# FFN stages: where ScalarE and VectorE split the coming weight blocks, inside the up loop and through its last turns

## The reference, cut to what matters

```python
def conv_ffn(h, w_up, conv_w, conv_b, w_down):
    u = h @ w_up                                  # 1024 -> 5632 columns
    u = lax.conv_general_dilated(u, conv_w[:, None, :], window_strides=(1,),
                                 padding=[(CONV_WIDTH - 1, 0)], ...) + conv_b   # width 3, per channel
    a, b = u[..., :D_FF], u[..., D_FF:]           # D_FF = 2816
    return (jax.nn.silu(a) * b) @ w_down          # 2816 -> 1024

x = x + conv_ffn(rms_norm_2(x, ffn_norm[l]), w_up[l], conv_w[l], conv_b[l], w_down[l])
```

## Time and profile before

| what | value |
|---|---|
| time, median of 3 runs | 1364.01 us (1361.56 to 1366.23) |
| the profiled execution's own time | 1362.08 us |
| its span, first to last instruction | 1360.2 us |
| mean granted TensorE clock | 0.912 |
| PE / PEld busy | 85% / 79% of the span |
| DVE / ACT / POOL busy | 70% / 51% / 9% |
| first FFN, about | 797 to 992 us from the span's start |
| second FFN, about | 1152 to 1347 us |

### The profile page before, as it was taken

One profiled execution on the slowest core, in us unless ns is written; L12 is line 12 of the kernel. 1 busy time (PEld: TensorE's weight loads), 2 busy tenths in 40 slices (PEclk: granted clock), 3 DMA queues, 4 the chain that ended last, 5 costly groups with the idle time before them and its releaser, 6 DMA issues.

```text
span 1360.2 us, 24905 instructions
## 1 busy us (share of the span) xinstructions
PE 1153.7 (85%) x10397; PEld 1071.4 (79%) x10397; DVE 945.8 (70%) x1723; ACT 697.5 (51%) x1256; POOL 118.2 (9%) x126
## 2 busy tenths in 40 slices
PE   6799866888899669579957799998978859999986
PEld 6688765888788659577945699998977849999886
DVE  5787955667879646676768668877558476778852
ACT  5642256546422465545437656565434464565551
POOL 2000000110000001141000011110011001011100
PEclk9999976989899869889958999998988979999988
DMA  8332111344321005425510145554634303454550
GB/s 337 118 111 77 64 63 32 120 159 148 124 94 66 32 5 191 147 73 195 175 62 1 63 156 183 162 183 161 219 112 159 124 1 127 153 182 162 173 182 31
DMA packets 24448, 167.55 MB, mean 123 GB/s; under 512 B 2704, under 2 KB 2832, under 8 KB 8208
## 3 DMA queue, kind: packets, MB, share of 16 engines
q1 hardware_dynamic: 24336, 165.96, 35.1%
HBM read 164.90 MB, written 1.05 MB: 122 GB/s over the span
## 4 chain that ended last, share of the span: by engine, by line
PE 42%; DVE 35%; ACT 16%; issue 5%; DMA 1%; POOL 1%; POOLq 0%; DVEq 0%; SPq 0%; ACTq 0%
DVE WL L381 8%; PE ps L427 8%; PE ps L422 8%; PE ps L424 8%; DVE ARENA L2033 5%; DVE FR L381 4%; ACT WH L368 4%; PE ps L445 3%; PE ps L453 2%; PE ps L447 2%; ACT ARENA L745 2%; ACT FR L368 2%; PE ps L643 2%; DVE ARENA L2025 2%; ACT L484 2%
## 5 line engine op out<-in xcount | busy, mean ns | idle before, releaser
L381 DVE TENSOR_TENSOR WL<-raw,WH 128x1024 fp32r<-128x1024 f32 (+4 forms) x225 | 262.9, 1191 | 138.0 <-ACT WH L368 137.5
L422 PE MATMUL ps<-FR,WH 128*128 128x256 f32 x1248 | 310.9, 288 | 26.4 <-ACT WH L368 20.4
L424 PE MATMUL ps<-FR,WH 128*128 128x256 f32 x1248 | 307.4, 286 | 1.9 <-POOL FR L501 1.0
L368 ACT ACTIVATE WH<-raw 128x1024 fp32r<-128x1024 f32 (+4 forms) x225 | 217.5, 989 | 111.2 <-PE ps L427 64.4
L422 PEld LDWEIGHTS ps<-FR,WH 128*128 128x128 f32 x1248 | 244.1, 196 | 32.0 <-ACT WH L368 17.8
L424 PEld LDWEIGHTS ps<-FR,WH 128*128 128x128 f32 x1248 | 243.8, 195 | 4.4 <-POOL FR L501 2.1
L422 PE MATMUL ps<-FR,FR 128*128 128x256 f32 x680 | 170.3, 287 | 6.9 <-ACT FR L368 6.3
L427 PE MATMUL ps<-FR,WL 128*128 128x256 f32 x1248 | 170.6, 279 | 0.3 <-DVE WL L381 0.3
L424 PE MATMUL ps<-FR,FR 128*128 128x256 f32 x680 | 169.2, 286 | 0.2 <-DVE FR L493 0.2
L381 DVE TENSOR_TENSOR FR<-raw,FR 128x1024 fp32r<-128x1024 f32 (+2 forms) x100 | 117.2, 1193 | 73.5 <-ACT FR L368 73.5
L427 PEld LDWEIGHTS ps<-FR,WL 128*128 128x128 f32 x1248 | 156.6, 190 | 0.6 <-DVE WL L381 0.6
(11 more groups left out here) (309 smaller groups left out, 1789.7 us busy)
## 6 DMA issues: line engine op xcount, KB each, us to landing
raw<-wst_in SPq DMA_DIRECT2D x124, 1024.0 KB, 5.0
raw<-wst_in SPq DMA_DIRECT2D x14, 768.0 KB, 4.3
raw<-wst_in SPq DMA_DIRECT2D x11, 896.0 KB, 4.8
raw<-wst_in SPq DMA_DIRECT2D x4, 968.0 KB, 4.7
raw<-wst_in SPq DMA_DIRECT2D x2, 912.0 KB, 4.6
cst<-cst_in SPq DMA_DIRECT2D x1, 1681.0 KB, 15.3
X<-xT_in SPq DMA_DIRECT2D x2, 512.0 KB, 6.4
ARENA<-memT_in SPq DMA_DIRECT2D x1, 1024.0 KB, 4.8
```

Of the source, the lines that this page charges most:

```text
L368: a.activation(hi[:, 0:cols], src, ACT.Copy).then_inc(*put("split_hi", ("hi", i)))
L381: v.tensor_tensor(lo[:, 0:cols], src, hi[:, 0:cols].bitcast(F32), SUB).then_inc(*put("split_lo", ("lo", i)))
L422: pe.matmul(out, hv[:, k, :], src.hi[:, c, :], start=k0 == 0 and k == ks[0], stop=False)
L424: pe.matmul(out, hv[:, k, :], src.lo[:, c, :], start=False, stop=False)
```

## The change

Inside the up loop ScalarE's two roundings of a turn are taken apart. Apart from the first call ahead of turn 0, which stays as it was, one item (2i+7) is rounded right behind the centre taps of turn i, ahead of `part_hi` and silu (`ahead` is 4 there), and the other (2i+8) at the end of the turn. VectorE's two remainders stand at the end of turn i instead of the beginning of turn i+1, which is the same place in its queue. The calls are no longer limited to i < 22: through new marks of the plan after each of the first four products of down, turns 21 to 24 go on to split items 49 and 50, 51 and 52, 53 and 54, 55 and 56, in the same two places of ScalarE's turn.

```diff
@@ def ffn_pe(l)
             for c in range(4):
                 feat("w_down_2", l, r(128 * c, 128 * c + 128), m.F, ("F", l), first[c][:, 0:256], "down1", l, c, kc=FC, span=span)
+                if span[0] == 0:
+                    B.at_items["up", l, FC + c] = len(B.plan)
@@ def ffn_v(v, q, l)
         for i in range(FC + 3):
             if i < FC:
-                split_lo(v, q, "up", l, i)
                 if i == 0:
+                    split_lo(v, q, "up", l, i)
                     barrier(q, "V", ("P", l))
...
                 part_lo(v, q, "part_lo_v", m.F, ("F", l), n, m.fb[n % 3])
+            split_lo(v, q, "up", l, min(i + 1, FC + 3))
@@ def ffn_a(a, q, l)
         for i in range(FC + 3):
             if i < FC:
-                split_hi(a, q, "up", l, i)
                 if i == 0:
+                    split_hi(a, q, "up", l, i)
                     barrier(q, "A", ("P", l))
...
                                  bias=vcol("conv_b_2", l, c), scale=vcol("conv_w_2", l, 88 + c)).then_inc(*put("ffn_a", ("centre", l, i)))
+            split_hi(a, q, "up", l, min(i + 1, FC + 3), ahead=NW + NMORE - 2)
             if 0 <= i - 2 < FC:
...
                 a.activation(u, u, ACT.Silu).then_inc(*put("ffn_a", ("silu", l, n)))
+            split_hi(a, q, "up", l, min(i + 1, FC + 3))
```

## The result

The changed kernel takes 1350.11 us (median of 4 runs, 1348.27 to 1353.01) against 1363.7 before (4 runs): a ratio of 0.990, 95% interval 0.988 to 0.993. The forecast was 1349.2 in 1341 to 1356. Its profiled execution has a span of 1347.2 us, 13.0 less than before.

A forecast was written before the change was run, and what follows sets the result against it. The prediction took TensorE's wait for item 49 behind each up loop, and the low clock after it, as the bound. Gaining 7.4 us in each FFN, 14.8 together, brings 1364.0 to 1349.2 us, range 1341 to 1356.

The forecast's parts named there:

- The place of the loss: Behind the up loop, TensorE waits 5.31 us for item 49, then runs at clock 0.55; 5.55 us wait in second FFN.
- The wait for `part_hi`: In each loop turn VectorE's `part_lo` waits 0.70 to 0.80 us, starting at 3.10 behind u instead of 2.30.
- The product's cost: In each loop turn GpSimd's product, no longer in VectorE's idle time, costs VectorE 0.50 us, making the period 6.21.
- rival 1: In the loop, the product costs VectorE nothing: period 5.71, 10.6 us gained in each FFN, 1342.8 us; chance 0.22.
- Who comes first: In the loop, GpSimd's product starts at 3.46 behind u, 0.03 us behind the start of VectorE's first remainder.
- rivals 2 and 3: In the loop: product costs more, 1353.4 or 1358.4 us, chance 0.18; product holds up both remainders, 1373.6 us, chance 0.04.
- Where item 49 stands: Rounded in turn 21 at u(21) + 2.8, item 49 ends 7.4 us earlier: 4.9 earlier start, 2.5 clock.
- The tail: Behind item 49 in down, nothing stops TensorE: items 50 onward are ready with margins of 1 to 3 us.
- rival 4: Behind the loop, TensorE stops at items 50 to 53, turn 22 being longer; half the gain goes, 1356.6 us; chance 0.06.
- The sum: Over the whole kernel, 7.4 us gained in each FFN, 14.8 together, everything else unchanged: median 1349.2 us.

The follow-up runs named there:

- e2: The changed kernel with the middle rounding alone, without the further splitting of items in turns 21 to 24: 1366.6 us, ratio 1.002.
- e1: The changed kernel without the middle rounding: both roundings stay together at the end of ScalarE's turn, splitting goes on through turns 21 to 24: 1344.9 us, 0.986.
- e3: The changed kernel with the middle rounding moved behind `part_hi`, in front of silu: 1340.5 us, ratio 0.983.
- e4: The changed kernel with GpSimd's product waiting for the turn's second remainder, so that it runs beside u: 1339.7 us, ratio 0.982.
- e6: The changed kernel with each GpSimd product computed twice into the same place: 1349.3 us, ratio 0.989.
- e7: The changed kernel with the splitting going on in turn 21 only, not in turns 22 to 24: 1360.0 us, ratio 0.997.
- e5: The changed kernel with both the middle rounding behind `part_hi` and the product beside u: 1340.4 us, ratio 0.983.

## Why the prediction was right

**The place of the loss.** Right: the stall in front of item 49 and the low clock behind it were what the change could win. e2 keeps both and gains nothing, e1 removes them and gains more than the whole change.

**The wait for `part_hi`.** Forecast 0.70 to 0.80 us, measured 0.72, `part_lo` at 3.10 behind u as forecast. e3 takes it away.

**The product's cost.** The term 0.50 measured 1.76 - 1.22 = 0.54, and made the period 6.26 instead of 6.21. That it had to be paid at all was read from two places of the trace before that lie outside the ordinary turns of the loop. e4 shows that the cost goes when the product is moved away from the remainders, and e6 that a second product beside u is free. Without it rival 1 would have been the forecast, 1342.8, 7 us too low; its period of 5.71 is what e4 shows, 5.72, where the product is out of the way.

**Who comes first.** The forecast put GpSimd 0.03 us behind the first remainder; it was 0.01. The tie went the same way in each of the 40 turns from 2 to 21 of the two FFNs, by 0.00 to 0.01 us, and rivals 2 and 3 did not come about. Had GpSimd been first, the cost would, as an estimate from the earlier trace rows, have been about the same; no run of the loop shows that order.

**Where item 49 stands.** It is rounded by u(21) + 2.8, as forecast. Mis-sized: the gain up to item 49 is 6.04 us, not 7.4. It starts 3.89 us earlier, where 4.9 was forecast: 19 x 0.05 = 0.95 of that is the period. And it takes 3.11 us (938.56 to 941.67) instead of 2.8. The wait for its remainder is at most 0.1 of these 0.3: its last eight matmuls take 1.17 us, those of item 2 took 1.10. The forecast put 2.8, the step from the end of one item to the end of the next, for the time from first start to last end; item 47, which also begins behind a short wait, takes 3.13. TensorE had caught up with the roundings at item 37, not 41.

**The tail.** Right that TensorE waits nowhere behind item 49 in down: the stretch to item 67 takes 45.0 us, against 44.5 before. e7 puts a price on a stop there, the outcome of rival 4 though from another cause: 5.1 us a stage without the splits of turns 22 to 24.

**The sum.** 14.8 us were forecast. The two stages give 12.2 up to item 49 (6.04 and 6.14), the spans 13.0, the medians 13.6. That the total is nearer to the forecast than its terms is luck. Most of what the stages do not give lies in one place between the two FFNs, from the last matmuls of line 643 to item 2 of the second FFN: 1159.26 - 1123.63 = 35.63 us before, 1152.93 - 1119.05 = 33.88 in the changed kernel, with another granted clock in its first 8 us. First PE and the stretch (columns as in the earlier trace rows) of before, then of the changed kernel:

```profile
1123.63 1.97 PE L643 MATMUL ps<-ARENA 128*64 128x128 f32 x16 [0.88 <-DVE ARENA L706]
1123.60:1131.60 8.00, 7.97 (x61) 7.67 (x62) 2.73 (x3) 2.51 (x3) 0.00 (x0) 0.76 0.00 0
...
1119.05 1.10 PE L643 MATMUL ps<-ARENA 128*64 128x128 f32 x16 [0.88 <-DVE ARENA L706]
1119.00:1127.00 8.00, 7.95 (x76) 7.81 (x77) 3.57 (x4) 2.94 (x5) 0.00 (x0) 1.00 0.10 13
```

The change does not decide this by itself. The profiles of e3, e4 and e5, which have its tail, show 0.76 to 0.77 and 35.6 to 36.0 us there, as before and e2 do; e1, e6 and e7 show 1.00 and 33.9 to 34.2, as the changed kernel does. What decides it is open. In e1's profile it makes up 1.4 of the 4 us that lie outside the two stages.

## What to carry to other kernels

Where a stream of prepared operands is split between loop turns and an epilogue, look first at the item that waits for the epilogue: here one stall of 5 us and the clock behind it, twice, were worth 14.7 us in the two stages (e1), and a better order inside the loop as well another 2 x (179.6 - 176.4) = 6.4 (e3, e4, e5). Moving a step forward on one engine to end the idle time of another can be paid twice: by what is queued behind the step on its own engine (here `part_hi`, 0.72 us), and by what used to lie in the idle time that is gone (here a GpSimd product, 0.54 us), together more than the 1.10 us won. So after such a move ask what the idle time was hiding. In this kernel the remedy was to put the two-operand GpSimd instruction beside a VectorE instruction that reads one operand from PSUM.

## What the runs showed of the hardware

A GpSimd tensor_tensor of 128x256 (0.74 us alone) that was issued 0.01 us behind a VectorE tensor_tensor of 128x1024 with two SBUF inputs left that one at 1.22 us and made the next one 1.76. Beside a VectorE instruction with one PSUM and one SBUF input (0.68 us) neither was longer (e4). The Trainium skill, page "SBUF — State Buffer", section "Who interferes with whom", says that whichever of the two issues first holds the shared ports for the whole instruction while the other is blocked, and that a VectorE instruction with at most one SBUF input, outside the 2-port modes, does not contend. The runs agree with both, with one size beside it: VectorE lost 0.54 us of the product's 0.74, so the hold is shorter than the product's record.

The granted clock of TensorE was 1.00 from 900 to 942 us of the changed kernel, with waits of 0.2 to 0.3 us in front of seven items. The wait of 3.55 us in e7 was followed by an item of 4.55 us (clock 0.66 over 951 to 956), and the 5.31 us of before by one of 5.26 (0.55 over 942 to 947).
